# High-weight products first: splitting TensorE's wait inside a weight panel

## What is computed

```python
def swiglu(h, w_gu, w_down):
    g, u = jnp.split(h @ w_gu, 2, axis=-1)
    return (jax.nn.silu(g) * u) @ w_down
...
    merged = g[:, :, 0] * ya + g[:, :, 1] * yb + g[:, :, 2] * yc + g[:, :, 3] * yd
    return merged @ w_o
```

## Time and profile before

| | |
|---|---|
| timed runs, us | 4662.50, 4665.16, 4669.51 |
| span of the profiled execution, us | 4668.2 |
| TensorE matmul busy | 4184.8 us, 90% |
| weight loads | 3826.0 us, 82% |
| VectorE busy | 2249.5 us, 48% |
| ScalarE busy | 1933.5 us, 41% |
| GpSimd busy | 2690.7 us, 58% |
| mean granted TensorE clock | 0.947 of full |

### The profile page before, as it was taken

The page is one execution under the profiler, slowest core; times in us unless marked ns, Lnnn a source line. Parts: engine busy times, 40 slices in busy tenths (PEclk is TensorE's granted clock), DMA queues, the critical chain, the costliest instruction groups (busy, mean ns, idle before and its releaser), DMA issues.

```text
span 4668.2 us, 94914 instructions
## 1 busy us (share of the span) xinstructions
PE 4184.8 (90%) x36305; PEld 3826.0 (82%) x36305; DVE 2249.5 (48%) x3002; ACT 1933.5 (41%) x2635; POOL 2690.7 (58%) x1186
## 2 busy tenths in 40 slices
PE   6898898899799889799999987999789999998898
PEld 5555898898589745598999977999689899987798
DVE  4423523543753452363636175635836355338463
ACT  2211445443344321154544454544644444435453
POOL 4000685576167500177778755777377787865576
PEclk9999999999799999899999998999899999999899
DMA  5344464455146434356556634555255565643454
GB/s 151 101 135 133 140 184 118 117 172 142 34 135 183 128 109 133 104 162 180 158 160 175 173 111 128 162 153 161 74 158 172 152 176 168 178 141 102 128 164 138
DMA packets 1177107, 664.37 MB, mean 142 GB/s; under 512 B 30141, under 2 KB 1138441, under 8 KB 1176743
## 3 DMA queue, kind: packets, MB, share of 16 engines
q1 hardware_dynamic: 1176871, 661.06, 49.0%
HBM read 659.92 MB, written 1.05 MB: 142 GB/s over the span
## 4 chain that ended last, share of the span: by engine, by line
PE 71%; issue 13%; POOL 7%; DVE 5%; ACT 2%; SPq 1%; DMA 1%; POOLq 0%; DVEq 0%; ACTq 0%
PE bank L634 54%; POOL wlo L539 7%; PE bank L963 5%; PE bank L714 2%; PE bank L614 1%; PE bank L1061 1%; PE bank L1055 1%; PE bank L797 1%; PE bank L1032 1%; DVE RSTD L720 1%; DVE W L736 1%; PE bank L870 1%; PE bank L1063 1%; DVE HL L787 1%; PE bank L1038 0%
## 5 line engine op out<-in xcount | busy, mean ns | idle before, releaser
L539 POOL TENSOR_TENSOR wlo<-raw,whi 128x1024 fp32r<-128x1024 f32 (+3 forms) x1182 | 2690.5, 2292 | 1953.7 <-ACT whi L549 1945.1
L634 PE MATMUL bank<-AH,whi 128*128 128x256 f32 x6320 | 1836.8, 291 | 190.0 <-DVE AL L692 104.0
L634 PE MATMUL bank<-AL,whi 128*128 128x256 f32 x6320 | 1818.5, 288 | 0.0
L634 PE MATMUL bank<-AH,wlo 128*128 128x256 f32 x6320 | 1817.3, 288 | 0.0
L549 ACT ACTIVATE whi<-raw 128x1024 fp32r<-128x1024 f32 (+3 forms) x1182 | 1171.2, 993 | 1277.2 <-PE bank L634 1134.1
L634 PEld LDWEIGHTS bank<-AH,whi 128*128 128x128 f32 x6320 | 1242.9, 197 | 208.2 <-issue 179.2
L634 PEld LDWEIGHTS bank<-AL,whi 128*128 128x128 f32 x6320 | 1246.2, 197 | 0.1
L634 PEld LDWEIGHTS bank<-AH,wlo 128*128 128x128 f32 x6320 | 1244.3, 197 | 0.0
L787 DVE TENSOR_TENSOR HL<-hid,HH 128x256 f32 x242 | 589.3, 2435 | 31.3 <-DVE HH L785 2.9
L634 PE MATMUL bank<-HH,whi 128*128 128x256 f32 x1936 | 548.0, 283 | 43.2 <-DVE HL L787 43.2
L634 PE MATMUL bank<-HL,whi 128*128 128x256 f32 x1936 | 546.2, 282 | 0.0
(11 more groups left out here) (334 smaller groups left out, 4167.8 us busy)
## 6 DMA issues: line engine op xcount, KB each, us to landing
raw<-in_ffn_w SPq DMA_DIRECT2D x420, 512.0 KB, 3.9
raw<-in_w_in SPq DMA_DIRECT2D x182, 512.0 KB, 3.8
raw<-in_ffn_w_gu SPq DMA_DIRECT2D x176, 512.0 KB, 3.8
raw<-in_w_ada SPq DMA_DIRECT2D x144, 512.0 KB, 3.8
raw<-in_ffn_w_down SPq DMA_DIRECT2D x64, 512.0 KB, 4.1
raw<-in_rw_w_rkv SPq DMA_DIRECT2D x48, 512.0 KB, 4.0
raw<-in_ffn_w SPq DMA_DIRECT2D x56, 384.0 KB, 3.5
raw<-in_ds_w_in SPq DMA_DIRECT2D x28, 512.0 KB, 3.7
```

Of the source, the lines that this page charges most:

```text
L539: pool.tensor_tensor(wlo[slot][:, 0:n], raw[slot][:, 0:n], whi[slot][:, 0:n], ALU.subtract).then_inc(lo_ready, 1)
L634: mm = pe.matmul(ps[:, 0:o.shape[2]], w, o[:, k0 + c, :], start=tile not in started and c == n == 0, stop=last_panel and c == nk - 1 and n ...
```

## The change

In `step` the loop over chunks is cut in two. The first loop runs, chunk by chunk, the two products with the high weights, behind a wait for `hi_ready` alone; the second runs the products with the low weights for all chunks, behind the wait for `lo_ready`. In the first panel of a chunked projection the wait for the operand's chunk stays in the first loop. In `tokens_step` a wait for `hi_ready` is added ahead of that for `lo_ready` and the order stays. The loops' counts take `hi_ready` in.

```diff
--- before.py
+++ after.py
@@ -602,6 +602,7 @@
 
                 for k, (_, _, k0, nk, _, (oh, ol)) in enumerate(g.panels):
                     slot = (g.p0 + j * g.pps + k) % RING
+                    pe.wait_ge(hi_ready, after(pe, hi_ready))
                     pe.wait_ge(lo_ready, after(pe, lo_ready))
                     for tt in range(TT):
                         if k == 0:
@@ -624,22 +625,26 @@
                     ps = bank[(g.t0 + j * g.tiles + tile) % RING]
                     if tile not in started:
                         free_bank()
-                    pe.wait_ge(lo_ready, after(pe, lo_ready))
+                    pe.wait_ge(hi_ready, after(pe, hi_ready))
                     last_panel = tile not in [x[4] for x in g.panels[k + 1:]]
                     for c in range(nk):
                         if chunked and isinstance(s, int) and s == k == 0:
                             pe.wait_ge(operand_ready, after(pe, operand_ready))
-                        wh, wl = (t[slot][:, c * P:(c + 1) * P] for t in (whi, wlo))
-                        for n, (w, o) in enumerate(((wh, oh), (wh, ol), (wl, oh))):
-                            mm = pe.matmul(ps[:, 0:o.shape[2]], w, o[:, k0 + c, :], start=tile not in started and c == n == 0,
-                                           stop=last_panel and c == nk - 1 and n == 2)
+                        w = whi[slot][:, c * P:(c + 1) * P]
+                        for n, o in enumerate((oh, ol)):
+                            pe.matmul(ps[:, 0:o.shape[2]], w, o[:, k0 + c, :], start=tile not in started and c == n == 0,
+                                      stop=False)
+                    pe.wait_ge(lo_ready, after(pe, lo_ready))
+                    for c in range(nk):
+                        mm = pe.matmul(ps[:, 0:S], wlo[slot][:, c * P:(c + 1) * P], oh[:, k0 + c, :], start=False,
+                                       stop=last_panel and c == nk - 1)
                     started.add(tile)
                     mm.then_inc(panels_done, 1)
 
             if by_hand:
                 return lambda s: step(s, s % g.body)
             n = g.body * g.pps
-            steps_of(pe, g, {bank_free: RING, lo_ready: n}, step, peel=chunked)
+            steps_of(pe, g, {bank_free: RING, hi_ready: n, lo_ready: n}, step, peel=chunked)
 
 
         def dve_tiles(dve, name, take, per=None, by_hand=False):
```

## The result

The changed kernel takes 4686.5 us as the median of five runs (4679.0 to 4700.4), the kernel before 4663.9 us beside it (4662.5 to 4669.5). The ratio is 1.0037, with a 95% interval from 1.0019 to 1.0054: slower, by some 9 to 25 us.

What follows compares the result with a forecast made beforehand. TensorE, streaming matmuls for 90% of the span, was taken as the bound. From 4665.2 us, 23.8 us lost at seventeen starts less 12.0 gained at eleven stalls gave 4677 us, the case's own range 4663 to 4694.

Steps and rivals of the forecast that it cites:

- The added waits: 1182 more waits on TensorE's queue, one per panel, cost 0 us in the closed matmul stream.
- the new order: High products before low ones in each panel, same matmuls at the same interval: 0 us, ends 133 us either way.
- The two rivals of a changed stream: Main projections get denser, -133 us, chance 0.04; or the mid-panel wait exposes weight loads, up to +233 us, chance 0.04.
- The eleven stalls: TensorE's eleven waits for GpSimd's low part, 11.4 us together, shorten: gain 12.0 us, ends 4 and 12.9.
- The rival by which the stalls only move: In paired projections a saved stall returns at the next panel: gain 4, sum +19.8, 4685 us; chance 0.12.
- The deferred products: In seventeen chunk-by-chunk projection starts, five chunks' low products move behind VectorE's pace: 0.60 us lost per start.
- The clock: Thinner TensorE work in the seventeen starts delays full clock: 0.80 us lost per start, ends 0 and 1.59.
- The rival by which the clock does not care: TensorE's activity in the seventeen starts suffices for the same grant: -1.8 us in all, 4663 us; chance 0.15.
- The sum: Whole kernel: loss 23.8 us minus gain 12.0 us gives +11.8 us, 4677 us, range 4663 to 4694.

Runs made afterwards that it cites:

- the experiment with the starts alone: New order only in the first panel of the seventeen chunk-by-chunk starts, old order elsewhere, against the kernel before: 4693.4 us, ratio 1.0063.
- the first experiment: The change everywhere except the first panel of the seventeen chunk-by-chunk starts, which keeps the old order, against the kernel before: 4657.1 us, ratio 0.9977.
- the throwaway kernel: Changed kernel plus one unread matmul per chunk in the first panel of the seventeen starts: 4666.6 us, ratio to the kernel before 0.9999.
- both waits first: New order in all panels, but the low-part wait also ahead of the high products: 4695.9 us, ratio to the kernel before 1.0060.
- The experiments with throwaways ahead: Unread matmuls before the first chunk of the seventeen starts; with 18, ratio to the kernel before 1.0000 in old order, 1.0058 in new order.
- the two kernels with three matmuls per chunk: 18 throwaway matmuls ahead of old-order starts; other panels in old order (ratio to the kernel before 1.0000) or new order (4659.1 us, 0.9976).
- the dense start: Changed kernel with each start's first two panels run together in old order, six matmuls per chunk: 4649.2 us, ratio to the kernel before 0.9955.

## Why the prediction was right, point by point

**The added waits and the new order: 0 each, right.** The stretch of 192 matmuls in the earlier trace rows takes 23.01 us between its first and last start, 23.00 before. The two rivals of a changed stream are out.

**The eleven stalls: right, somewhat under-sized.** I gave them 12.0 us, with 12.9 as the upper end; the trace shows 14.6. At most places 1.25 us are gained where I counted 1.13: the matmul behind a stall lasts 0.39 us and not 0.28, the next one starts 0.22 us behind it and not 0.12, and these 0.10 us go with the stall. The 0.3 us that I took off for stalls beyond 1.92 us went as well (the longest distance, 2.33 us, is 0.12 now); the experiment with the starts alone shows that the starts' own delay covers these. The rival by which the stalls only move is out: they are gone in the wait list of the changed kernel and of the first experiment.

**The deferred products: 0.60 us per start, right.** The smallest difference of all seventeen starts between the traces is 0.60 us, at one where the clock rose at the same time, and the throwaway kernel needs the same 0.60 to add up. Start by start, 0.60 + 0.44 x (half clock more) meets the difference within 0.03 us in twelve. In five this sum is off, from 0.46 us too high to 0.27 too low, and these are the ones where in one of the traces the clock was still full at the first chunk and fell 0.1 to 1.2 us later.

**The clock: right in kind and sign, slightly low.** I took 0.80 us per start, half of a spread of rises; the half clock grew by 2.14 us on average, times 0.44 is 0.93. With the 0.60 that is 1.53 beside the 1.54 measured, and the same two terms give 1.47 for the starts alone (measured 1.45) and 1.59 for both waits first (1.58). The largest difference of a single start, 2.33 us, lies a little over the 2.19 that I gave as the end. The rival by which the clock does not care is refuted by the throwaway per chunk, which adds activity to TensorE and takes away no work, and brings the loss down by 0.4%. By the Trainium skill (TensorE: Matmul & The Clock Gate, "What's actually happening") activity releases the throttle; the runs agree, with 4.98 us of half clock per start against 7.36.

**The sum.** +11.8 us foretold; the traces say +11.6 for the two terms, 26.2 - 14.6, and the ratio 9 to 25 us. That the sum is so close is luck: the loss was 2.4 us under-sized and the gain 2.6, and they cancel. The median of 4686.5 us is inside the range I gave but 9.5 us over the point. I did not reckon with the spread between runs, which grew: 4679 to 4700 for the changed kernel in the first comparison. Starts of one kernel differ by up to 1.8 us with the moment at which the clock rises, and over 29 runs of the kernel before (4658 to 4688 us) the longer ones had the lower mean granted clock: 2.7 us for 0.001 of it, with a correlation of -0.67. So the clock has a part in the spread; whether it is all of it was not tried.

**What I had not seen.** I priced the half clock, but took the state at the start as given. The clocks of 0.53 and 0.54 in the earlier trace rows already said that two of the three starts shown came at full clock and lost it right behind the first chunk: their 7.31 and 3.67 us are times to the rise and hold 6.83 and 3.41 us of half clock. The experiments with throwaways ahead show that a full clock is mostly lost within the start when VectorE paces it (in 13 and 16 of 17 in the two kernels with three matmuls per chunk, in all with two), and more often kept with denser work (lost in 6 of 17 with six).

## What to carry to other kernels

Before moving work behind other work, look at the places where it lay in somebody else's time: here it was seventeen panels of 1182, and they cost more than the eleven stalls that the change removed. Where an engine is paced by another one at the start of a stage, fill the gaps with work that is due anyway (a second tile on the same operand) rather than thin it out; on TensorE this pays twice, since the full clock then comes earlier or holds. Throwaway matmuls ahead of such a start are worth nothing alone and 0.5% with the dense start behind them.

## What the runs showed of the hardware

- Thin work costs the full clock, with gaps far under a microsecond. Behind the same 18 throwaways the starts that were at full clock throughout are none of 17 with two matmuls per 0.73 us, 4 and 1 with three (two kernels), and 11 with six. In one with two it fell from 1.00 to 0.50 some 2 us into the start, after 2.27 us of standing; in the same start with six it held for all 11.55 us. The standing ahead has its part: with 32 throwaways all 17 held.
- A third matmul per chunk whose result nobody uses made the kernel faster by 0.4%, by bringing the full clock 2.4 us earlier on average.
- A microsecond at half clock costs 0.44 us only where TensorE is the bound. With the throwaways ahead and the old order the starts had half the half clock of before (2.61 and 5.22 us) and were 0.23 us shorter, not 1.15: what was saved lay where VectorE set the pace.
- Waits and register operations between matmuls are free in a closed stream: a stretch of 192 matmuls with eight waits more changed by 0.01 us.
